# A transposed operand made by VectorE in blocks of 32 and four-way moves through DRAM, where TensorE multiplied by the identity

## The chip, the cores and the metric

The kernel runs on one core of one Trainium2 chip. The metric is the device time of one launch in microseconds (us), and the median of three runs is quoted. TensorE does the matrix products (PE in the rows), VectorE (DVE) and ScalarE (ACT) work elementwise, and SyncE (SP) issues nearly all DMA transfers, in one queue and in program order.

## The reference

One decoder layer with two token mixers, 256 tokens by 2048 features, all in float32. What matters here is its end:

```
ya = jnp.einsum('bsc,cd->bsd', oa * jax.nn.silu(ga), w_o_a[l])
yb = jnp.einsum('bsc,cd->bsd', ob * jax.nn.silu(gb), w_o_b[l])
merged = jax.nn.sigmoid(ma) * ya + jax.nn.sigmoid(mb) * yb
x = x + jnp.einsum('bsd,de->bse', merged, w_out[l])
```

`ya` and `yb` are products over 1024 features, the last product is over all 2048 features of `merged`.

## The kernel before

Every large product is made of **units**. A unit takes two blocks of 128 rows of a weight matrix, 512 columns wide, and multiplies them with both halves (128 tokens each) of the transposed activations. Each float32 operand is split into a high part `hi` and a rest `lo` (both of type fp32r), and hi·hi + hi·lo + lo·hi is added up, so that a unit is 2 x 2 x 3 = 12 products of 128x128 with 128x512. The weights of a unit pass through one of four slots: SP loads `raw` (512 KB), ACT rounds it to `hi`, DVE subtracts to get `lo`, TensorE multiplies. ACT makes `hi` of unit u after the product of unit u-4 is done; DVE makes `lo` of unit u after that; SP loads unit u after the `lo` of unit u-4.

The **tail** of the kernel has 64 units, called 0 to 63 below (the code adds `U_O`). Units 0 to 31 are the two projections, `projections(n)` for column chunk n = 0 to 3: units 8n to 8n+3 for `w_o_a`, 8n+4 to 8n+7 for `w_o_b`. When unit 8n+7 is done, DVE multiplies the second gate in and adds both parts (`gate_b_and_merge(n)`), which gives 512 columns of `merged` in `stage`, tokens on partitions. The last product wants these transposed, features on partitions: `merged_steps` multiplies the eight blocks of 128x128 with the identity on TensorE (into PSUM banks T0 and T0+1), ACT rounds them to `hT_hi` (`merged_hi`), DVE subtracts to `hT_lo` (`merged_lo`). Units 32 to 63 are the product with `w_out`; unit 32+8m+i reads blocks 2i and 2i+1 of `hT_hi` and `hT_lo`, so that chunk n of `merged` is read first by unit 32+2n, and the last chunk (n = 3) by unit 38.

Nothing is scheduled by a planner. Each engine has its own instruction list, written out by hand, and takes it strictly in order; semaphores with a count join them. `split_hi` and `split_lo` count the finished pieces of `hT_hi` and `hT_lo`, `lo_ready` the units whose weights are ready, `unit_done` the finished units.

Of the kernel before, what the change touches and what calls it, by code (L numbers as in the profile page):

```python
# [25 lines left out]
ACT = mybir.ActivationFunctionType  # L26
# [4 lines left out]
P = 128  # L31
# [12 lines left out]
IDX_SCALE = IDX_HEADS ** -0.5 * IDX_DIM ** -0.5  # L44

CW = 512
X_CUTS = (0, 1, 2, 4, 6, 8, 10, 12, 14, 16)
X_FRONT = KT + HD // 2
EARLY = 3
# [84 lines left out]
def build_layer(nc, x, x_columns, positions, w_in, a_q_gain, a_k_gain, b_q_gain, b_k_gain,  # L134
# [4 lines left out]
    with ExitStack() as ctx:  # L139
# [13 lines left out]
        def sem(name):  # L153
            return ctx.enter_context(nc.semaphore(name))
# [64 lines left out]
        swapped = sb("swapped", [P, RT, CW])  # L219
        swapped_r = sb("swapped_r", [P, RT, CW], F32R, at=swapped_at)  # L220

        QB_COLS = 3 * P
        work_flat = [stage[:, :, :].rearrange("p r n -> p (r n)"),
                     roped[:, :, :].rearrange("p r n -> p (r n)"),
# [98 lines left out]
        merged = sem("merged")  # L323
        last_pieces, rest_added = sem("last_pieces"), sem("rest_added")

        dve_wrote = sem("dve_wrote")
# [5 lines left out]
        def _(sp):  # L332
# [64 lines left out]
            def load_projections(n):  # L397

                for b, weights in enumerate((w_o_a, w_o_b)):
                    for i in range(4):  # L400
                        load(i, n * 8 + (U_O + 4 * b + i), weights, 2 * i, n * CW)

            load_projections(0)
            sp.wait_ge(split_lo, 16)
            sp.dma_start(g[:, :, :], x_rows).then_inc(res_landed, 16)
            with sp.Fori(1, 4) as n:
                load_projections(n)
            with sp.Fori(0, 4) as n:
                for i in range(CK):
                    load(i % RING, n * CK + (U_W + i), w_out, 2 * i, n * CW)  # L410
            for n in range(3):
# [103 lines left out]
        def _(pe):  # L515
# [59 lines left out]
            def transpose_step(rows, bank):  # L575

                for b in range(2):
                    for r in range(RT):
                        o = ps[:, bank, b * S + r * P:b * S + (r + 1) * P]
                        ins = nc.tensor.transpose(o.bitcast(F32R), rows(b, r), ident_r[:, :])  # L580
                ins.then_inc(split_T, 1)
# [133 lines left out]
                    w_in_unit(c, i, chunk_bank(c))  # L715


            def merged_steps(n):

                pe.wait_ge(merged, n + 1)  # L720
                pe.wait_ge(split_lo, n * 2 + 16)
                for half in range(2):
                    transpose_step(lambda b, r: stage_r[:, r, (2 * half + b) * P:(2 * half + b + 1) * P], T0 + half)

            def projections(n):

                for branch in range(2):
                    for i in range(4):
                        first = isinstance(n, int)
                        if not first and branch == 0 and i == 2:  # L730
                            merged_steps(n - 1)
# [42 lines left out]
                projections(n)  # L774
            for n in range(4):
                for i in range(CK):
                    if n == 0 and i == 2:
                        merged_steps(3)
                    if i == 0:
                        pe.wait_ge(tail_out, 6 + n + 1)  # L780
                    if n == 0 and i in (0, 6, 7):
                        pe.wait_ge(split_lo, {0: 22, 6: 23, 7: 24}[i])
                    if n < 3 or i < CK - RING:
                        unit(U_W + CK * n + i, i % RING, 2 * i, hT_hi, hT_lo, 2 * (n % 2), i == 0, i == CK - 1)
            last_units()
# [3 lines left out]
        def _(act):  # L789
# [4 lines left out]
            def split_hi_step(t, dst, k0, bank):  # L794

                act.wait_ge(split_T, t - 7)
                activation(dst[:, bass.ds(k0, 2), :], ps[:, bank, :].rearrange("p (k s) -> p k s", k=2),
                           ACT.Copy).then_inc(split_hi, 1)
# [213 lines left out]
            def merged_hi(n, half):  # L1012
                t = n * 2 + half
                split_hi_step(t + 16, hT_hi, t * 2, T0 + half)

            def tail_hi_ahead(n, i):

# [4 lines left out]
                tail_hi_ahead(0, i)  # L1022
            with act.Fori(1, 5) as n:
                for i in range(8):
                    if i in (2, 3):
                        merged_hi(n - 1, i - 2)
                    tail_hi_ahead(n, i)
            for n in range(5, 8):
                for i in range(8):
# [9 lines left out]
        def _(dve):  # L1039
# [290 lines left out]
            def gate_b_and_merge(n):  # L1330

                dve.wait_ge(unit_done, n * 8 + (U_O + 8))
                a_part, b_part = (m[:, :, bass.ds(n * CW + b * D, CW)] for b in range(2))
                tt(b_part, ps[:, 2:4, :], b_part, ALU.mult).then_inc(tail_out, 1)
                dve.wait_ge(tail_out, n * 2 + 2)
                dve.wait_ge(split_T, n * 2 + 8)
                tt(stage[:, :, :], a_part, b_part, ALU.add).then_inc(merged, 1)

            def merged_lo(n, half):
                t = n * 2 + half  # L1340
                split_lo_step(t + 16, hT_lo, hT_hi, t * 2, T0 + half)

            def tail_lo_ahead(n, i):
                make_lo(n * 8 + (U_O + i + RING), i % RING)
# [7 lines left out]
            with dve.Fori(1, 4) as n:  # L1352
                for i in range(8):
                    if i == 0:
                        gate_b_and_merge(n - 1)
                    if i in (2, 3):
                        merged_lo(n - 1, i - 2)
                    if i == 4:
                        gate_a(n)
                    tail_lo_ahead(n, i)  # L1360
            for n in range(4, 8):
                for i in range(8):
                    u = U_O + 8 * n + i
                    if n == 4 and i == 0:
                        gate_b_and_merge(3)
                    if n == 4 and i in (2, 3):
                        merged_lo(3, i - 2)
# [45 lines left out]
```

## Time and profile before

| what | value |
|---|---|
| median of 3 runs | 797.82 us (797.64 to 798.22) |
| span of the profiled execution, first to last instruction | 796.4 us |
| TensorE busy | 792.7 us, 100% of the span |
| VectorE busy | 481.5 us, 60% |
| ScalarE busy | 418.4 us, 53% |
| DMA, mean | 192 GB/s, 152.92 MB |
| granted TensorE clock | 1.000 of full speed throughout |

The span is what the profiler saw between the first and the last instruction. The page gives no other time for this execution; the median of the three runs is 1.4 us above the span, which is what lies outside it. Products overlap in the trace (each is shown with some 390 ns although one starts every 227 ns), so TensorE's rate is read from the distance between starts.

### The profile page before, as it was taken

The numbers are of one execution on the slowest core, as the hardware profiler recorded it, in microseconds if no ns is written. First come the engines' busy times: TensorE is split into PE (matmuls) and PEld (weight loads), VectorE is DVE, ScalarE is ACT, GpSimd is POOL, SyncE is SP. The second block draws the span as 40 slices with busy tenths as digits, with TensorE's granted clock in tenths as the row PEclk, the third lists the DMA queues.
The fourth block names the chain that finished last, engine by engine and source line by source line (L and its number), as shares of the span: only waits on it lengthen the run. The fifth ranks groups of instructions, "written<-read, shape, count | busy, mean of one in ns | idle before, by whom it ended". The sixth has DMA issues, their size and how long they took to land.

```text
span 796.4 us, 10773 instructions
## 1 busy us (share of the span) xinstructions
PE 792.7 (100%) x3810; PEld 667.3 (84%) x3810; DVE 481.5 (60%) x663; ACT 418.4 (53%) x670; POOL 46.8 (6%) x70
## 2 busy tenths in 40 slices
PE   9999999999999999999999999999999999999998
PEld 9998888888888888888888888888888888888887
DVE  7677766666677554668656455555455566665453
ACT  7574556665555454556465554555575444443431
POOL 4341000000000000000000000000000000000000
PEclk9999999999999999999999999999999999999999
DMA  9986665666666565666655665655665855555563
GB/s 316 313 264 198 186 187 168 183 199 180 199 187 187 171 194 162 196 189 193 177 154 173 166 176 161 185 160 172 173 185 182 293 195 184 185 194 189 187 194 122
DMA packets 81082, 152.92 MB, mean 192 GB/s; under 512 B 5136, under 2 KB 12944, under 8 KB 80784
## 3 DMA queue, kind: packets, MB, share of 16 engines
q1 hardware_dynamic: 80752, 152.06, 62.8%
q8 instruction: 25, 0.41, 0.2%
q10 hardware_dynamic: 288, 0.30, 0.1%
q14 instruction: 17, 0.14, 0.0%
HBM read 150.25 MB, written 2.10 MB: 191 GB/s over the span
## 4 chain that ended last, share of the span: by engine, by line
PE 97%; ACT 1%; DMA 1%; SPq 0%; issue 0%; DVE 0%; ACTq 0%
PE ps L527 30%; PE ps L529 30%; PE ps L528 29%; PE ps L538 2%; PE ps L569 1%; PE ps L580 1%; DMA raw<-in_w_in 1%; PE ps L638 0%; PE ps L749 0%; PE ps L748 0%; PE ps L747 0%; PE ps L646 0%; ACT L938 0%; ACT L832 0%; ACT g L832 0%; PE ps L626 0%
## 5 line engine op out<-in xcount | busy, mean ns | idle before, releaser
L1068 DVE TENSOR_TENSOR lo<-raw,hi 128x1024 fp32r<-128x1024 f32 (+2 forms) x279 | 335.2, 1204 | 290.2 <-ACT hi L819 288.4
L819 ACT ACTIVATE hi<-raw 128x1024 fp32r<-128x1024 f32 (+2 forms) x277 | 287.1, 1040 | 337.4 <-PE ps L529 323.8
L527 PE MATMUL ps<-hi,hT_hi 128*128 128x512 f32 (+2 forms) x936 | 364.3, 389 | 0.0
L529 PE MATMUL ps<-hi,hT_lo 128*128 128x512 f32 (+2 forms) x936 | 361.1, 386 | 0.0
L528 PE MATMUL ps<-lo,hT_hi 128*128 128x512 f32 (+2 forms) x936 | 360.8, 385 | 0.0
L529 PEld LDWEIGHTS ps<-hi,hT_lo 128*128 128x128 f32 x936 | 175.7, 188 | 35.1
L528 PEld LDWEIGHTS ps<-lo,hT_hi 128*128 128x128 f32 x936 | 175.8, 188 | 32.9
L527 PEld LDWEIGHTS ps<-hi,hT_hi 128*128 128x128 f32 x936 | 175.7, 188 | 33.0
L527 PE MATMUL ps<-hi,ogT_hi 128*128 128x512 f32 x128 | 50.1, 391 | 0.0
L529 PE MATMUL ps<-hi,ogT_lo 128*128 128x512 f32 x128 | 49.8, 389 | 0.0
L528 PE MATMUL ps<-lo,ogT_hi 128*128 128x512 f32 x128 | 49.8, 389 | 0.0
L453 POOL TENSOR_SCALAR small<-small 128x8 f32<-128x8 f32 (+1 forms) x13 | 2.8, 212 | 504.2 <-ACT stage L999 318.4
L529 PEld LDWEIGHTS ps<-hi,ogT_lo 128*128 128x128 f32 x128 | 24.0, 188 | 5.0
L528 PEld LDWEIGHTS ps<-lo,ogT_hi 128*128 128x128 f32 x128 | 24.0, 188 | 4.9
L527 PEld LDWEIGHTS ps<-hi,ogT_hi 128*128 128x128 f32 x128 | 24.0, 188 | 4.9
L938 ACT ACTIVATE roped<-stage,small 128x128 f32<-128x128 f32 (+1 forms) x32 | 14.3, 446 | 13.0 <-DVE small L1206 13.0
L856 ACT ACTIVATE swapped<-stage 128x128 f32<-128x128 f32 x64 | 18.9, 297 | 0.3
L455 POOL TENSOR_TENSOR small<-small,half 128x8 f32<-128x8 f32 (+1 forms) x13 | 16.6, 1281 | 1.1
L1088 DVE TENSOR_TENSOR swapped<-stage,g 128x256 f32<-128x256 f32 (+2 forms) x44 | 16.2, 409 | 0.0
L1084 DVE TENSOR_TENSOR roped<-stage,g 128x512 f32<-128x512 f32 (+2 forms) x22 | 14.5, 660 | 0.0
L1092 DVE TENSOR_TENSOR roped<-roped,swapped 128x1024 f32<-128x1024 f32 (+2 forms) x11 | 12.3, 1121 | 0.0
L856 ACT ACTIVATION_READ_ACCUMULATOR swapped<-stage 128x1 f32 x64 | 12.0, 188 | 0.0
(167 smaller groups left out, 484.5 us busy)
## 6 DMA issues: line engine op xcount, KB each, us to landing
raw<-in_w_in SPq DMA_DIRECT2D x192, 512.0 KB, 3.8
raw<-in_w_out SPq DMA_DIRECT2D x32, 512.0 KB, 4.3
raw<-in_w_o_a SPq DMA_DIRECT2D x16, 512.0 KB, 3.7
raw<-in_w_o_b SPq DMA_DIRECT2D x16, 512.0 KB, 3.6
raw<-in_w_in SPq DMA_DIRECT2D x13, 384.0 KB, 5.3
raw<-in_w_in SPq DMA_DIRECT2D x8, 336.0 KB, 5.3
x_own<-in_x SPq DMA_DIRECT2D x4, 512.0 KB, 6.4
g<-in_x SPq DMA_DIRECT2D x1, 2048.0 KB, 10.3
```

What stands on the lines that cost most here:

```text
L455: return tt(out, mean, half[:, 0:width], ALU.pow)
L527: mm(o, a_hi, w_hi[:, j], start=first and j == 0, stop=False)
L528: mm(o, a_hi, w_lo[:, j], start=False, stop=False)
L529: ins = mm(o, a_lo, w_hi[:, j], start=False, stop=j == 1 and last)
L538: ins = mm(ps[:, chunk_bank(c) + r, 0:IDX_W[0]], stationary[:, 2 * unit_k + j, r * P:(r + 1) * P], moving[:, u % RING, j, 0:IDX_W[0]], sta ...
L819: activation(hi[:, slot, :, 0:width], raw[:, slot, :, 0:width], ACT.Copy).then_inc(hi_ready, 1)
L856: ins = activation(swapped[:, r, at], stage[:, r, at], ACT.Square, accum_out=ss_h[:, j:j + 1])
L938: ins = activation(probs[buf][:, at], masked[buf][:, at], ACT.Exp, scale=SCALE, bias=neg_max[:, j:j + 1], accum_out=sum_p[:, j:j + 1])
L1068: tt(lo[:, slot, :, 0:width], raw[:, slot, :, 0:width], hi[:, slot, :, 0:width].bitcast(F32), ALU.subtract).then_inc(lo_ready, 1)
L1084: mark(tt(cos_out[:, r], src[:, r], c_tab, ALU.mult))
L1088: mark(tt(sin_out[:, r, :, half_b], src[:, r, :, other], s_tab, ALU.mult))
L1092: tt(roped[:, :, 0:cols], roped[:, :, 0:cols], swapped[:, :, 0:cols], ALU.add).then_inc(rope_done, 1)
```

## The change

The eight identity products for each chunk, their PSUM banks and `merged_steps` go. After the sum, DVE transposes `stage` in blocks of 32x32 into `swapped` (one instruction over 128x1024). SP then writes `swapped` to a DRAM buffer (`keep_turned`, 512 KB), waits until it has landed, and reads it back in four transfers of 128 KB, one for each group of 32 partitions, in runs of 256 numbers, into `roped` (`bring_turned`). ACT and DVE make `hT_hi` and `hT_lo` from `roped`, in two pieces of 128x512 (one for each half of the tokens), before they turn to the weights of unit 8n+8 (for chunk n-1), i.e. two places later in their lists than before.

```diff
+            def keep_turned(n):
+                sp.wait_ge(merged_turned, n + 1)
+                sp.dma_start(turned_home, swapped[:, :, :].rearrange("p r n -> p (r n)")).then_inc(turned_kept, 16)
+
+            def bring_turned(n):
+                sp.wait_ge(turned_kept, 16 * n + 16)
+                for c in range(P // BLOCK):
+                    to = roped[c * BLOCK:(c + 1) * BLOCK, :, :].rearrange("j r n -> j (r n)")
+                    sp.dma_start(to.rearrange("j (q n) -> j q n", q=P // BLOCK), turned_rows[c]).then_inc(turned_back, 16)
+
+            def move_merged(n, i):
+                if n >= 0 and i == 0:
+                    keep_turned(n)
+                if n >= 0 and i == 1:
+                    bring_turned(n)
...
-            def merged_steps(n):
-
-                pe.wait_ge(merged, n + 1)
-                pe.wait_ge(split_lo, n * 2 + 16)
-                for half in range(2):
-                    transpose_step(lambda b, r: stage_r[:, r, (2 * half + b) * P:(2 * half + b + 1) * P], T0 + half)
-
...
-                    if n == 0 and i in (0, 6, 7):
-                        pe.wait_ge(split_lo, {0: 22, 6: 23, 7: 24}[i])
+                    if n == 0 and i in (0, 4, 6):
+                        pe.wait_ge(split_lo, {0: 20, 4: 22, 6: 24}[i])
...
+            def merged_hi(n):
+
+                act.wait_ge(turned_back, 64 * n + 64)
+                for r in range(RT):
+                    to = hT_hi[:, bass.ds(n * 4, 4), r * P:(r + 1) * P]
+                    activation(by_blocks(to), columns_of(roped, r), ACT.Copy).then_inc(split_hi, 1)
...
-                    if i in (2, 3):
-                        merged_hi(n - 1, i - 2)
+                    if i == 4:
+                        merged_hi(n - 1)
...
                 dve.wait_ge(tail_out, n * 2 + 2)
-                dve.wait_ge(split_T, n * 2 + 8)
                 tt(stage[:, :, :], a_part, b_part, ALU.add).then_inc(merged, 1)
+                dve.wait_ge(merged, n + 1)
+                nc.vector.transpose(swapped[:, :, :].rearrange("p r n -> p (r n)"),
+                                    blocks_of(stage)).then_inc(merged_turned, 1)
+
+            def merged_lo(n):
+
+                for r in range(RT):
+                    dve.wait_ge(split_hi, n * 2 + (17 + r))
+                    to, rounded = (t[:, bass.ds(n * 4, 4), r * P:(r + 1) * P] for t in (hT_lo, hT_hi))
+                    tt(by_blocks(to), columns_of(roped, r), by_blocks(rounded).bitcast(F32),
+                       ALU.subtract).then_inc(split_lo, 1)
```

SP's list, which was three loops over the tail, is now written out. These are its rows from the loads of units 32 and on, for the chunks n = 2 and n = 3. Before, two loads in a row of one loop (the wait, then the transfer):

```order
L353 ISA [waits lo_ready]
L353 DMA raw<-in_w_out 128x2x512
L351 REGISTER_ALU
L353 ISA [waits lo_ready]
L353 DMA raw<-in_w_out 128x2x512
```

And now, from the load of unit 32 to those after the last block move:

```order
L371 DMA raw<-in_w_out 128x2x512 [waits lo_ready]
L424 DMA turned<-swapped 128x1024 [waits merged_turned]
L371 DMA raw<-in_w_out 128x2x512 [waits lo_ready]
L430 DMA roped<-turned 32x4x256 [waits turned_kept]
L430 DMA roped<-turned 32x4x256 x3
L371 DMA raw<-in_w_out 128x2x512 [waits lo_ready] x7
L424 DMA turned<-swapped 128x1024 [waits merged_turned]
L371 DMA raw<-in_w_out 128x2x512 [waits lo_ready]
L430 DMA roped<-turned 32x4x256 [waits turned_kept]
L430 DMA roped<-turned 32x4x256 x3
L371 DMA raw<-in_w_out 128x2x512 [waits lo_ready] x22
```

For chunk 3 the write stands behind the load of unit 40, and the four reads behind the load of unit 41; the load of unit 42 stands behind them.

VectorE's list for the last chunk, from the gate product of chunk 3 on. Before:

```order
L1334 TENSOR_TENSOR m<-ps,m 128x2x512 [waits unit_done]
L1337 TENSOR_TENSOR stage<-m 128x1024 [waits split_T,tail_out]
L1068 TENSOR_TENSOR lo<-raw,hi 128x1024 [waits hi_ready] x2
L1054 TENSOR_TENSOR hT_lo<-ps,hT_hi 128x512 [waits split_hi]
L1068 TENSOR_TENSOR lo<-raw,hi 128x1024 [waits hi_ready]
L1054 TENSOR_TENSOR hT_lo<-ps,hT_hi 128x512 [waits split_hi]
L1068 TENSOR_TENSOR lo<-raw,hi 128x1024 [waits hi_ready] x5
```

And now:

```order
L1363 TENSOR_TENSOR m<-ps,m 128x2x512 [waits unit_done]
L1365 TENSOR_TENSOR stage<-m 128x1024 [waits tail_out]
L1367 STREAM_TRANSPOSE swapped<-stage 128x1024 [waits merged]
L1097 TENSOR_TENSOR lo<-raw,hi 128x1024 [waits hi_ready] x4
L1375 TENSOR_TENSOR hT_lo<-roped,hT_hi 128x4x128 [waits split_hi] x2
L1097 TENSOR_TENSOR lo<-raw,hi 128x1024 [waits hi_ready] x4
```

The block transpose stands ahead of the `lo` of unit 36, and both pieces of `hT_lo` between the `lo` of unit 39 and that of unit 40.

## Rows read from the trace of the kernel before

**Rows 1.** The page: the chain that ended last, by engine.

```profile
span 796.4 us, 10773 instructions
PE 792.7 (100%) x3810; PEld 667.3 (84%) x3810; DVE 481.5 (60%) x663; ACT 418.4 (53%) x670; POOL 46.8 (6%) x70
PE 97%; ACT 1%; DMA 1%; SPq 0%; issue 0%; DVE 0%; ACTq 0%
```

**Rows 2.** Timeline of TensorE, last chunk: start, duration, line, operation.

```profile
705.61 0.39 PE L527 MATMUL ps<-hi,hT_hi 128*128 128x512 f32 x1
...
711.06 0.81 PE L580 MATMUL ps<-ident_r,stage_r 128*128 128x128 f32 x8
...
718.61 0.39 PE L527 MATMUL ps<-hi,hT_hi 128*128 128x512 f32 x1
...
721.33 0.39 PE L527 MATMUL ps<-hi,hT_hi 128*128 128x512 f32 x1
...
722.69 0.39 PE L527 MATMUL ps<-hi,hT_hi 128*128 128x512 f32 x1
```

**Rows 3.** The chain in order of time: start, duration; first and last of four.

```profile
643.69 0.64 PE ps L580 x8
...
711.22 0.65 PE ps L580 x8
```

**Rows 4.** Timeline of VectorE around the last chunk.

```profile
706.90 1.23 DVE L1068 TENSOR_TENSOR lo<-raw,hi 128x1024 fp32r<-128x1024 f32 x1 [1.49 <-ACT hi L819]
708.05 1.22 DVE L1334 TENSOR_TENSOR m<-ps,m 128x1024 f32<-128x1024 f32 x1
709.30 1.23 DVE L1337 TENSOR_TENSOR stage<-m 128x1024 f32<-128x1024 f32 x1
710.44 1.22 DVE L1068 TENSOR_TENSOR lo<-raw,hi 128x1024 fp32r<-128x1024 f32 x1
...
716.97 0.68 DVE L1054 TENSOR_TENSOR hT_lo<-ps,hT_hi 128x512 fp32r<-128x512 f32 x1
```

**Rows 5.** Timeline of ScalarE around the last chunk.

```profile
711.25 1.06 ACT L819 ACTIVATE hi<-raw 128x1024 fp32r<-128x1024 f32 x1 [1.66 <-PE ps L529]
712.22 0.58 ACT L797 ACTIVATE hT_hi<-ps 128x512 f32 x1
```

**Rows 6.** Timeline of SP's queue: the issues of loads 40 and 41.

```profile
711.83 0.38 SPq L353 DMA_DIRECT2D raw<-in_w_out  x1
...
713.75 0.37 SPq L353 DMA_DIRECT2D raw<-in_w_out  x1
```

**Rows 7.** Instructions of tile raw, 705 to 740 us: the 13 loads, issue to landing.

```profile
DMA to landing us min/median/max: 3.4/4.2/4.5
```

**Rows 8.** DMA issues from 755 us on: count, KB each, us to landing.

```profile
out<-g SPq DMA_DIRECT2D x1, 256.0 KB, 2.2
...
out<-g SPq DMA_DIRECT2D x1, 128.0 KB, 1.9
```

**Rows 9.** DMA issues from 774 to 775.5 us, and from 775.5 to 777 us.

```profile
raw<-in_w_out SPq DMA_DIRECT2D x1, 512.0 KB, 5.0
out<-g SPq DMA_DIRECT2D x1, 512.0 KB, 5.2
...
out<-g SPq DMA_DIRECT2D x1, 512.0 KB, 6.1
```

**Rows 10.** Busy time by stretch: us, PE, PEld, DVE, ACT, POOL, clock, DMA share, GB/s.

```profile
4.00:10.00 6.00, 5.92 (x32) 5.49 (x32) 4.40 (x9) 4.27 (x10) 0.00 (x0) 1.00 1.01 341
793.00:794.00 1.00, 0.64 (x6) 0.44 (x4) 0.74 (x2) 0.00 (x0) 0.00 (x0) 1.00 0.00 0
794.00:795.00 1.00, 0.00 (x0) 0.00 (x0) 0.11 (x1) 0.00 (x0) 0.00 (x0) 1.00 0.40 136
795.00:796.00 1.00, 0.00 (x0) 0.00 (x0) 0.00 (x0) 0.00 (x0) 0.00 (x0) 1.00 0.37 126
```

**Rows 11.** Busy time, 688 to 710 us, the 22 us before the last chunk.

```profile
688.00:710.00 22.00, 22.00 (x104) 18.24 (x103) 14.09 (x14) 9.46 (x10) 0.00 (x0) 1.00 0.54 181
```

More of the change, by code:

```diff
@@ L46 @@
 CW = 512
+BLOCK = 32
 X_CUTS = (0, 1, 2, 4, 6, 8, 10, 12, 14, 16)
@@ L220, in build_layer, with blocks_of, columns_of, by_blocks @@
         swapped_r = sb("swapped_r", [P, RT, CW], F32R, at=swapped_at)
+        turned_home = nc.dram_tensor("turned", (P, RT * CW), F32, kind="Internal").ap()
+        turned_rows = turned_home.rearrange("(q j) (c n) -> c j q n", j=BLOCK, c=P // BLOCK)
+        def blocks_of(t):
+            return t[:, :, :].rearrange("p r (b c i) -> p c (r b) i", c=P // BLOCK, i=BLOCK)
+        def columns_of(t, r):
+            return t[:, :, :].rearrange("p r n -> p (r n)").rearrange("p (q r b i) -> p r b q i", q=P // BLOCK, r=RT,
+                                                                      i=BLOCK)[:, r]
+        def by_blocks(t):
+            return t.rearrange("p b (q i) -> p b q i", i=BLOCK)
         QB_COLS = 3 * P
@@ L322, in build_layer @@
         gates_ready = sem("gates_ready")
-        merged = sem("merged")
+        merged, merged_turned, turned_kept, turned_back = (sem("merged"), sem("merged_turned"), sem("turned_kept"),
+                                                           sem("turned_back"))
         last_pieces, rest_added = sem("last_pieces"), sem("rest_added")
@@ L401, in load_projections @@
                         load(i, n * 8 + (U_O + 4 * b + i), weights, 2 * i, n * CW)
+                        move_merged(n - 2, 4 * b + i)
+            def keep_turned(n):
[11 more added lines that the diff above has]
+                    bring_turned(n)
             load_projections(0)
@@ L405, in _ @@
             sp.dma_start(g[:, :, :], x_rows).then_inc(res_landed, 16)
-            with sp.Fori(1, 4) as n:
+            for n in range(1, 4):
                 load_projections(n)
-            with sp.Fori(0, 4) as n:
+            for n in range(4):
                 for i in range(CK):
                     load(i % RING, n * CK + (U_W + i), w_out, 2 * i, n * CW)
+                    if n < 2:
+                        move_merged(n + 2, i)
             for n in range(3):
@@ L729, in projections @@
                         first = isinstance(n, int)
-                        if not first and branch == 0 and i == 2:
-                            merged_steps(n - 1)
                         if i == 0 and first:
@@ L776, in _ @@
                 for i in range(CK):
-                    if n == 0 and i == 2:
-                        merged_steps(3)
                     if i == 0:
                         pe.wait_ge(tail_out, 6 + n + 1)
-                    if n == 0 and i in (0, 6, 7):
-                        pe.wait_ge(split_lo, {0: 22, 6: 23, 7: 24}[i])
+                    if n == 0 and i in (0, 4, 6):
+                        pe.wait_ge(split_lo, {0: 20, 4: 22, 6: 24}[i])
                     if n < 3 or i < CK - RING:
@@ L1010, in _ @@
                     make_hi_ahead(c, i)
-            def merged_hi(n, half):
-                t = n * 2 + half
-                split_hi_step(t + 16, hT_hi, t * 2, T0 + half)
+            def merged_hi(n):
[3 more added lines that the diff above has]
+                    activation(by_blocks(to), columns_of(roped, r), ACT.Copy).then_inc(split_hi, 1)
             def tail_hi_ahead(n, i):
@@ L1335, in gate_b_and_merge @@
                 dve.wait_ge(tail_out, n * 2 + 2)
-                dve.wait_ge(split_T, n * 2 + 8)
                 tt(stage[:, :, :], a_part, b_part, ALU.add).then_inc(merged, 1)
-            def merged_lo(n, half):
-                t = n * 2 + half
-                split_lo_step(t + 16, hT_lo, hT_hi, t * 2, T0 + half)
+                dve.wait_ge(merged, n + 1)
[7 more added lines that the diff above has]
+                       ALU.subtract).then_inc(split_lo, 1)
             def tail_lo_ahead(n, i):
@@ L1355, in _ @@
                         gate_b_and_merge(n - 1)
-                    if i in (2, 3):
-                        merged_lo(n - 1, i - 2)
                     if i == 4:
                         gate_a(n)
+                        merged_lo(n - 1)
                     tail_lo_ahead(n, i)
@@ L1365, in _ @@
                         gate_b_and_merge(3)
-                    if n == 4 and i in (2, 3):
-                        merged_lo(3, i - 2)
+                    if n == 4 and i == 4:
+                        merged_lo(3)
                     if n >= 5 and i == 0:
```

## Prediction

> **What bounds the kernel now.** I read the page first: TensorE is busy 100% of the span and carries 97% of the chain that ended last [rows 1]. So time is saved only by taking work out of TensorE's stream, and lost only where TensorE is made to wait. Next I read TensorE's own timeline in the tail for its pace. A unit of 12 products starts at 718.61 and the next at 721.33 [rows 2]: 2.72 us a unit, 227 ns a product, with no gap. Then the other engines in the last iteration before the change's critical place: over 22 us VectorE is busy 14.09, ScalarE 9.46, the DMA engines 54% [rows 11]. Each has room on average; whether the new chain of steps fits is a question of its length, not of these shares.
>
> **What is taken away.** Eight identity products for each of four chunks. The chain gives them 0.64 to 0.65 us for eight [rows 3], but the products behind them are also paced a little slower for a while. The honest price is the distance between repeats. The first and last of the four groups start at 643.69 and 711.22 [rows 3]: 67.53 us for three iterations, 22.51 each, where eight units take 8 x 2.72 = 21.76. So a group costs 0.75 us, and four give back **3.0 us**. They do lie on the path, since nothing else is on TensorE at those times. The same comes out at the last group: unit 32 starts at 705.61, so unit 38 would start at 705.61 + 6 x 2.72 = 721.93, and it starts at 722.69 [rows 2], 0.76 later.
>
> The Trainium skill (VectorE: DVE Perf Modes, Rules for kernel authors and The three transpose paths) speaks against the change: transpose 128x128 blocks on TensorE if the result may lie in PSUM, as it did here. Its figure for one such product on TensorE is 390 ns, for bf16. By it 32 products would cost 12.5 us, and the kernel would come out near 788 with the stall below. The starts in rows 2 and 3 are closer than that by four times (0.65 us for eight), so I give that outcome no more than 0.01.
>
> **What is added, and who waits for it.** A chain: block transpose on VectorE, write to DRAM, read back, `hT_hi`, `hT_lo`, and then TensorE. For the chunks n = 0 to 2 TensorE reads the result an iteration or more later, so their latency itself is hidden. The last chunk is first read by unit 38, six units after the sum can begin. That is the place where the end is set. I write it in the times of the trace before, with unit 32 starting at T = 705.61 [rows 2]; the three groups saved earlier only shift T.
>
> 1. VectorE: `lo` of unit 35 from 706.90, gate product 708.05, sum 709.30 to 710.53 [rows 4], as before.
> 2. Block transpose. No row shows one. The nearest are VectorE's operations over 128x1024 f32, 1.22 us [rows 4]. I take 1.2, with a start 0.1 after the sum ends: done at 711.85. Bounds: 0.6 if it ran at twice that pace, 2.4 if it took two passes.
> 3. `lo` of unit 36 follows, to 713.1 instead of 710.44 + 1.22 = 711.66. SP issues the load of unit 40 behind it; before, this came 0.17 after the end of `lo` (711.83) and took 0.38 [rows 6]. So the load goes out at 713.25 and the write, next in the queue, at 713.65. The wait for `merged_turned` is long over by then. The load of unit 41 moves from 713.75 [rows 6] to some 714.4; it is not late, since its `hi` waits for unit 37.
> 4. Write of 512 KB. Two rows with less and nothing ahead of them: 1.9 us for 128 KB, 2.2 for 256 KB [rows 8], which at 0.3 for each 128 KB makes 2.8 for 512 KB. Of full size, right behind a load as here: 5.2, and 6.1 with another write ahead [rows 9]. I take 4.8, a little under the row that is nearest, since the load ahead of that one was itself slow (5.0 against a median of 4.2 [rows 7]). Landed at 718.45; bounds 2.8 and 6.1.
> 5. Four reads of 128 KB, issued from 718.55. SP needs some 0.35 for each issue (0.37 for a load [rows 6]), so the last goes out 1.05 after the first. Loads of 512 KB in one piece land after 3.4 to 4.5, median 4.2 [rows 7]. The runs are 1 KB, where the write's are 4 KB; but runs of 1.5 KB at the kernel's start still moved 341 GB/s [rows 10], so I don't slow them, and take 4.2: all four landed at 722.75. Bounds 3.4, and 5.1 if the moved bytes (half of a load's time) took twice as long.
> 6. ScalarE: two copies of 128x512, 0.58 each [rows 5], 722.85 to 724.0. VectorE: the second `hT_lo` behind it, 0.68 [rows 4], to **724.75**. Both engines are free: the `lo` of unit 39 is done by some T + 13.5.
>
> TensorE wants unit 38's operands at 721.93. It stands still for **2.8 us**. Sum: -3.0 + 2.8 = -0.2 us. Against the profiled execution: 796.4 - 0.2 = 796.2 of span, and with the 1.4 us by which the median stands above that span 797.6.
>
> **What is queued behind the waits.** SP waits at the first read for the write to land, up to 718.55, and issues the four reads to 719.9. Loads 42 and 43 stand behind; 42 goes out at 719.9. Its `hi` may begin when unit 38 is done, after 724.6 and now later still, and 719.9 + 4.2 = 724.1: not late. ScalarE waits for the reads before the `hi` of unit 40. Here is the second place: in the iterations n = 1 to 3 the same wait stands ahead of the `hi` of unit 8n+8, which TensorE wants 8 units = 21.76 us after T. Reads landed at T + 17.14, two copies (1.15), `hi` of unit 8n+8 (1.06), `lo` (1.23) and the hand-overs: ready at T + 20.65. **Slack 1.1 us.** The unit after it has 2.72 more to spend and costs ScalarE 1.06, so it has no stall. I cost this place at nothing; the cover is this 1.1 us, and every microsecond beyond it costs one in each of three iterations besides the one at unit 38. VectorE's transposes themselves (4 x 1.2) are hidden in its idle time; the block product delays the `lo` of unit 8n+4 by 1.3, which TensorE wants at T + 10.9 and which is done at T + 7.5. The chunk's gates are read from PSUM before the transpose, so no bank comes free later. The unrolled loops of SP cost nothing on TensorE's path.
>
> **The clock.** Granted clock is 1.00 to the end [rows 10], which is the 2.4 GHz level. After the last product at 793.6 TensorE does nothing, and the clock still stands at 1.00 in the slice up to 796.00, 2.4 us later. A stall of 2.8 us is about as far as any row reaches. If it fell to 1.2 GHz behind the stall, each unit at that level would take up to 5.4 instead of 2.72; one such unit would add 2.7 us. That belongs to the slower outcomes.
>
> **The rivals.**
>
> - *No change that can be told, as above:* a stall of 1.4 to 4.6 us at unit 38 against 3.0 saved, 796.2 to 799.4. A difference under 0.2% (1.6 us) is about what a measurement of this kernel can't tell from none. Chance 0.51.
> - *Faster, transfers are quick:* both land at the ends nearest to what a transfer can do alone. Write 3.4 (2.8 and 0.6 for the load ahead), reads 3.4: the end is 2.2 us earlier, the stall 0.6, and the sum -2.4: 795.4. It decides when the two transfers together take less than 7.6 us. For it: loads landed in as little as 3.4 (the lowest of rows 7); against it: the write follows a load by 0.4 us, and four separate reads must all land. Chance 0.15. The Trainium skill (DMA: Bandwidth & Descriptors, Anatomy of one DMA) gives about 2.0 us fixed and then 436 GB/s, for transfers that GpSimd issues. By it 512 KB take 3.2 us, both 6.4 instead of 9.0; the stall would be 0.2 us and the median 795.0. In this tail no load of 512 KB landed in less than 3.4 [rows 7] and no write of that size in less than 5.2 [rows 9].
> - *Slower, ScalarE's wait for the block reads starves TensorE in every iteration:* write 6.1 and reads 5.1, landed at T + 19.3. Then `lo` of unit 8n+8 is ready at T + 22.8, 1.1 us late in each of three iterations, and unit 38 waits 5.0: -3.0 + 3.3 + 5.0 = +5.3, 803.1. It starts to count from T + 18.2 and turns the result slower by 0.2% when the reads land some 1.3 us later than I take, at T + 18.4 (-0.2 + 1.3 + 3 x 0.2 = +1.7). For it: six hand-overs between engines and queues, of which I gave most 0.1 us or nothing; 1 KB pieces; loads, write and reads share one queue at 54% load. Chance 0.27.
> - *Slower, one term is larger:* the block transpose takes 2.4 (everything is 1.2 later, stall 4.0, and the slack overdrawn by 0.1 in three iterations: +1.3), and with it the clock falls for a unit or two: 799 to 802. Chance 0.06.
> - *The identity products were not worth their distance:* TensorE's stream is no shorter without them, because the same time goes to something that they hid. The stall then stands alone: +2.8, 800.6. Nothing in rows 2 shows such cover. Chance 0.01.
>
> **How the numbers follow.** The likeliest is the sum, 797.6. Its own range is 796.2 to 799.4. The range that should hold 8 of 10 reaches down to the quick transfers, 795.4, and up into the starved iterations, short of their far end: 802.0. Faster 0.15, same 0.51, slower 0.34 (0.27 + 0.06 + 0.01).
>
> **What the profile after would show.** Identity products on `stage` gone, four iterations 21.76 us apart (22.51 before) if no stall is in them. One gap on TensorE before unit 38, released by VectorE's `hT_lo`, of 2 to 4 us. Block transpose about 1.2 us. Write landing in 4.8, the reads in 4.2 from the first issue. ScalarE's longest wait in the tail for `roped`, near 5 us in each iteration. The prediction fails if the transfers take under 7.6 or over 10.3 us together, or if the `hi` of unit 8n+8 comes so late that TensorE also waits at the start of an iteration.

## The result and the profile after

The changed kernel takes 803.15 us (median of 4, 802.72 to 804.86) against 797.73 us before (median of 4): ratio 1.0071, 95% interval 1.0057 to 1.0086. It is 5.4 us slower; the forecast was no change, with a range that ended at 802.0. The profiled execution is the longest of the four: 804.86 us, span 803.0. The one before was the longest of its four too: 798.22 us, span 796.4 [rows 1].

The page after, its busy times, the granted clock by fortieths of the span, the chain that ended last, and TensorE's idle time in two groups (behind the bar: busy, mean ns of one; then the idle time before them and its releaser):

```profile
span 803.0 us, 10549 instructions
PE 793.4 (99%) x3778; PEld 666.5 (83%) x3778; DVE 485.9 (61%) x667; ACT 417.9 (52%) x670; POOL 46.8 (6%) x70
PEclk9999999999999999999999999999999999998999
PE 87%; DMA 5%; DVE 3%; ACT 2%; issue 2%; SPq 1%; DVEq 0%; ACTq 0%
L564 PE MATMUL ps<-hi,hT_hi 128*128 128x512 f32 (+2 forms) x936 | 365.7, 391 | 4.2 <-DVE hT_lo L1375 4.0
L564 PE MATMUL ps<-hi,ogT_hi 128*128 128x512 f32 x128 | 50.0, 391 | 1.6 <-DVE lo L1097 1.6
```

TensorE held 97% of the chain before; now 87%, and DMA 5%. One slice of the clock is lower. The first product of the tail, all gaps of TensorE in it and the products around the last one, from its timeline (start, duration, in brackets the idle time before and what ended it):

```profile
615.97 0.39 PE L564 MATMUL ps<-hi,ogT_hi 128*128 128x512 f32 x1
...
661.10 0.50 PE L564 MATMUL ps<-hi,ogT_hi 128*128 128x512 f32 x1 [1.45 <-DVE lo L1097]
...
683.32 0.50 PE L564 MATMUL ps<-hi,ogT_hi 128*128 128x512 f32 x1 [0.16 <-DVE lo L1097]
...
705.66 0.47 PE L564 MATMUL ps<-hi,hT_hi 128*128 128x512 f32 x1 [0.28 <-DVE lo L1097]
...
721.87 0.39 PE L566 MATMUL ps<-hi,hT_lo 128*128 128x512 f32 x1
726.21 0.80 PE L564 MATMUL ps<-hi,hT_hi 128*128 128x512 f32 x1 [3.95 <-DVE hT_lo L1375]
726.81 0.63 PE L565 MATMUL ps<-lo,hT_hi 128*128 128x512 f32 x1
727.23 0.63 PE L566 MATMUL ps<-hi,hT_lo 128*128 128x512 f32 x1
...
732.35 0.41 PE L566 MATMUL ps<-hi,hT_lo 128*128 128x512 f32 x1
732.60 0.40 PE L564 MATMUL ps<-hi,hT_hi 128*128 128x512 f32 x1
```

The reader is to see three things. First, the three gaps at the starts of units 16, 24 and 32 have used up what three groups of identity products gave back (2.25 us): unit 32 starts at 705.66, before at 705.61 [rows 2]. The brackets give 1.89 us for the three, but they count from the modelled end of the product before, 0.39 after its start, where the next product would start after 0.227. By the starts, units 0 to 31 took 89.69 us here (615.97 to 705.66) and 87.04 in the kernel without the trip, shown below: 2.65 lost. Second, the gap at unit 38: without it this unit would start 0.23 after 721.87, at 722.10; it starts at 726.21, 4.1 later. Third, behind the gap the products start 0.60 and then 0.42 to 0.43 apart instead of 0.227, until 732.35. Busy times by stretch (the third column from the right is the clock) say why:

```profile
724.00:726.00 2.00, 0.00 (x0) 0.00 (x0) 1.13 (x2) 1.80 (x3) 0.00 (x0) 0.88 0.99 347
726.00:728.00 2.00, 1.79 (x4) 1.49 (x5) 1.83 (x3) 1.25 (x2) 0.00 (x0) 0.50 0.28 100
728.00:730.00 2.00, 2.00 (x6) 1.52 (x5) 0.69 (x1) 0.00 (x0) 0.00 (x0) 0.50 0.58 187
730.00:732.00 2.00, 2.00 (x6) 1.52 (x6) 0.00 (x0) 0.26 (x1) 0.00 (x0) 0.50 0.82 259
732.00:734.00 2.00, 2.00 (x10) 1.62 (x9) 1.17 (x1) 0.80 (x1) 0.00 (x0) 0.91 0.20 78
```

The granted clock fell to 0.50 (1.2 GHz) while TensorE stood idle. From 726.21 to 732.60 fifteen products start; at 0.227 each that takes 3.4 us, here 6.39: **3.0 us** lost to the clock and the first product behind the gap. The account of this execution, all by starts: -3.0 (products gone) + 2.8 (gaps at iterations: 2.65, and 0.1 behind the start of unit 32, whose next product also comes late) + 4.1 + 3.0 - 0.4 (the tail began earlier, at 615.97 instead of 616.33) = +6.5. The last product starts 6.5 later than before (799.88, before 793.37), and the span is 6.6 longer.

The chain in order of time, from the sum of chunk 1 to the copies of chunk 3, with the longest pieces only (start, length, what):

```profile
665.73 1.24 DVE stage L1365
...
668.15 1.20 DVE lo L1097
669.78 5.75 DMA turned<-swapped
675.92 0.43 SPq L430
...
676.87 2.91 DMA roped<-turned
680.44 0.62 ACT hT_hi L1043
681.06 0.96 ACT hi L845
...
691.99 5.81 DMA turned<-swapped
...
714.14 5.73 DMA turned<-swapped
...
721.21 2.87 DMA roped<-turned
724.20 0.64 ACT hT_hi L1043
724.87 1.30 DVE hT_lo L1375 x2
```

The writes go out at 669.78, 691.99 and 714.14, some 22.2 us apart, where eight units take 21.76. (The first went out at 645.62, 24.2 before the second: its four reads took 6.4 us from the first issue to the copies, the other chunks' 4.3.) It is a loop of its own: the reads land, ScalarE and VectorE catch up on four units of weights, only then VectorE multiplies the next gate in, sums, transposes, and the next write goes out. The block transpose itself takes what was assumed:

```profile
704.29 4.63 DVE L1097 TENSOR_TENSOR lo<-raw,hi 128x1024 fp32r<-128x1024 f32 x4
708.84 1.22 DVE L1363 TENSOR_TENSOR m<-ps,m 128x1024 f32<-128x1024 f32 x1
710.09 1.23 DVE L1365 TENSOR_TENSOR stage<-m 128x1024 f32<-128x1024 f32 x1
711.34 1.25 DVE L1367 STREAM_TRANSPOSE swapped<-stage 128x1024 f32<-128x1024 f32 x1
```

### The profile page after: what moved, and what is told of

The parts are those of the page before. It is cut to its first block, busy times and chain, and to the rows that moved or that the text cites. A ratio compares the mean times of both kernels' runs of the same rounds, so it can differ in the third digit from the quotient of the medians.

```text
span 803.0 us, 10549 instructions
## 1 busy us (share of the span) xinstructions
PE 793.4 (99%) x3778; PEld 666.5 (83%) x3778; DVE 485.9 (61%) x667; ACT 417.9 (52%) x670; POOL 46.8 (6%) x70
## 4 chain that ended last, share of the span: by engine, by line
PE 87%; DMA 5%; DVE 3%; ACT 2%; issue 2%; SPq 1%; DVEq 0%; ACTq 0%
PE ps L564 26%; PE ps L566 26%; PE ps L565 26%; DMA turned<-swapped 3%; PE ps L575 3%; DMA roped<-turned 2%; DVE lo L1097 2%; PE ps L606 1%; ACT hi L845 1%; DVE stage L1365 1%; SPq L430 1%; DVE m L1363 1%; PE ps L623 1%; PE ps L675 0%; PE ps L777 0%
## 5 line engine op out<-in xcount | busy, mean ns | idle before, releaser
L1043 ACT ACTIVATE hT_hi<-roped 128x512 f32 x8 | 4.6, 624 | 27.2 <-DMA roped<-turned 27.2
L1375 DVE TENSOR_TENSOR hT_lo<-roped,hT_hi 128x512 f32 (+1 forms) x8 | 5.2, 688 | 21.8 <-ACT hT_hi L1043 21.8
```

## The experiments

Each is an edit of the changed kernel; times are medians, and ratios are to the kernel before, run on the same chip beside them (797.73, 798.27 and 798.15 us in the three groups of four). Differences to the changed kernel are to its 803.15 us; since the kernel before differs by up to 0.5 us between groups, they are no more exact than that, and the ratios go before them.

**Without the trip.** Left out are the write and the reads; the copies come from the block-transposed tile.

```diff
...
-                act.wait_ge(turned_back, 64 * n + 64)
+                act.wait_ge(merged_turned, n + 1)
...
-                    activation(by_blocks(to), columns_of(roped, r), ACT.Copy).then_inc(split_hi, 1)
+                    activation(by_blocks(to), columns_of(swapped, r), ACT.Copy).then_inc(split_hi, 1)
...
```

> The write and the four reads are left out; ScalarE and VectorE take their copies from the block-transposed tile itself, so blocks are not moved between partition groups and the last product works on wrongly placed numbers. Theory: the identity products are worth 3.0 us of TensorE's stream (four groups of 0.75), VectorE's block transposes are hidden, and all of the loss comes from the trip through DRAM. Then no TensorE gap is left in the tail, iterations are 21.76 us apart and the time is 797.7 - 3.0 = 794.7 (794.2 to 795.3). Rival: the stream without identity products is not shorter, or VectorE's transposes delay the weights: 797.5 or more, with gaps on TensorE behind lo.

Measured: 794.99 us, ratio 0.9965 (0.9952 to 0.9979). No gap of TensorE in the tail; the span is 793.4, 3.0 less than before (the medians differ by 2.7). Units 0 to 31 take 87.04 us, 32 times 2.72:

```profile
616.36 0.39 PE L561 MATMUL ps<-hi,ogT_hi 128*128 128x512 f32 x1
...
703.40 0.39 PE L561 MATMUL ps<-hi,hT_hi 128*128 128x512 f32 x1
```

The products were worth 3.0 us, and VectorE's transposes cost nothing. Everything lost is lost by the trip.

**The gap at unit 38 filled.** 18 products that nobody reads.

```diff
+                    if n == 0 and i == 6:
+                        for _ in range(18):
+                            mm(ps[:, T0, :], hT_hi[:, 0, 0:P], hT_hi[:, 0:2, :], start=True, stop=True)
                     if n == 0 and i in (0, 4, 6):
```

> 18 products of 128x128 with 128x512 into a PSUM bank that nobody reads are put on TensorE ahead of unit 38, which fill 18 x 0.227 = 4.1 us, the length of the gap there. Theory: behind the gap TensorE ran at 1.2 GHz for 14 products of 0.427 instead of 0.227 us, 2.8 us in all, and the first product after the gap took 0.37 longer; with the gap filled the granted clock stays at 1.00, and the time falls by 2 to 3.2 us to 800 to 801. Rival: only the wait itself costs, and the low clock is no more than a sign of it (or comes in any case): time as in the changed kernel, 803.1, or some tenths more.

Measured: 800.92 us (800.32 to 801.66), 2.2 less than the changed kernel; ratio 1.0038 (1.0025 to 1.0052). TensorE still waited after the filling, and the clock stayed up:

```profile
720.46 4.24 PE L809 MATMUL ps<-hT_hi 128*128 128x512 f32 x18
725.91 0.50 PE L564 MATMUL ps<-hi,hT_hi 128*128 128x512 f32 x1 [1.21 <-DVE hT_lo L1378]
```

So the low clock is a cost of its own, 2 to 3 us on top of the gap: 2.2 by the medians here, 3.0 by the starts in the profiled execution of the changed kernel. In this execution the last chunk's reads took 5.95 us and not 4.3, so that unit 38 waited longer than in the changed kernel (from 720.46 to 725.91, the filling counted in) and the clock still held. The Trainium skill (TensorE: Matmul & The Clock Gate, Why this matters for your kernels) warns of idle gaps between bursts of products, behind which, if they are long, the clock is back at half; the rows agree: it fell in a gap of 3.95 us and stayed up over the 1.21 that the filling left.

**Reads behind two more loads.**

```diff
-                if n >= 0 and i == 1:
+                if n >= 0 and i == 3:
                     bring_turned(n)
```

> SP issues the four block reads behind the loads of units 8n+10 and 8n+11 instead of ahead of them; they still go out soon after the write has landed. Theory: in the changed kernel the fourth read landed after 4.9 us where the first three took 2.7 to 2.9, because two loads of 512 KB are issued right behind it; with nothing behind the reads the fourth takes 2.8 to 3.2, all have landed some 4.5 us after the first issue instead of 6.3, the stall at unit 38 shrinks from 4.0 to about 2.2, the iterations' stalls go, and the time is 799 to 801. Rival: the reads are slow by themselves (1 KB rows, half of the partitions' ports), or the two loads, now ahead of them, cost them the same: 803 or later.

Measured: 816.61 us, ratio 1.0235 (1.0221 to 1.0249), 13.5 slower than the changed kernel. My theory for this run fell. I had read the fourth read's 4.9 us as the doing of the loads issued behind it; but that was the first chunk's, and in the other three the fourth read landed in 2.9 with the same loads behind it (the chain above). SP's queue and then ScalarE in one iteration of this kernel:

```profile
698.62 0.47 SPq L424 DMA_DIRECT2D turned<-swapped  x1
699.35 4.53 SPq L371 DMA_DIRECT2D raw<-in_w_out  x3
704.14 1.75 SPq L430 DMA_DIRECT2D roped<-turned  x4
```

```profile
711.23 1.15 ACT L1043 ACTIVATE hT_hi<-roped 128x512 f32 x2 [9.00 <-DMA roped<-turned]
```

From the first issue (704.14) to the last landing (711.2) 7.1 us pass, where the changed kernel needs 4.3 in three of its four chunks. What is *ahead* in the queue delays the reads: with three loads issued just ahead of them they took 6.8 to 8.0 us in the four chunks, though none was issued behind them before they had landed.

**Copies one place later.**

```diff
-                    if i == 4:
+                    if i == 5:
                         merged_hi(n - 1)
...
                         gate_a(n)
+                    if i == 5:
                         merged_lo(n - 1)
...
-                    if n == 4 and i == 4:
+                    if n == 4 and i == 5:
                         merged_lo(3)
```

> ScalarE's and VectorE's copies of the returned blocks stand one place later, behind hi and lo of unit 8n+8 instead of ahead of them. Theory: ScalarE's wait of up to 7.8 us for the reads no longer holds up the weights of unit 8n+8, so the gaps at the starts of iterations (1.45, 0.16, 0.28 us) go, and the write of the last chunk goes out 0.5 to 0.8 earlier; the stall at unit 38 stays, at 3.2 to 3.9. Time 800 to 801.3. Rival: the iterations' gaps come from late loads (SP's wait for the write ahead of loads 8n+10 and on), and stay: 802.5 to 803.5.

Measured: 800.95 us, 2.2 less; ratio 1.0038 (1.0024 to 1.0052). The gaps at iterations are gone; the one at unit 38 stays at its size, 3.0 us earlier than in the changed kernel:

```profile
723.25 0.80 PE L564 MATMUL ps<-hi,hT_hi 128*128 128x512 f32 x1 [3.94 <-DVE hT_lo L1375]
```

The gaps at iterations came from the place of the copies in two lists, not from late loads. The first chunk's reads took 6.4 us here too, and one place later in the lists that cost TensorE nothing.

**Write ahead of the load.**

```diff
+                        if b == 0 and i == 0 and n >= 2:
+                            keep_turned(n - 2)
                         load(i, n * 8 + (U_O + 4 * b + i), weights, 2 * i, n * CW)
...
-                if n >= 0 and i == 0:
-                    keep_turned(n)
...
+                    if n < 2 and i == 0:
+                        keep_turned(n + 2)
                     load(i % RING, n * CK + (U_W + i), w_out, 2 * i, n * CW)
```

> The write is issued ahead of the load of unit 8n+8 instead of behind it. Theory: it goes out when the block transpose is done, 1.5 to 2 us sooner, with no load ahead of it; the reads follow, the iterations' gaps go (1.9 us in all), the stall at unit 38 falls from 4.0 to 2.0 to 2.5, and the clock may stay up. Time 797 to 799.5. Rival: the write takes its 5.7 us whatever is ahead of it and the reads now meet the load behind it (6 us or more from first issue to last landing): a gain of 1.5 us or less, 801 or later.

Measured: 802.61 us (801.71 to 805.32), ratio 1.0061 (1.0047 to 1.0076) against 1.0071 (1.0057 to 1.0086): no gain that can be told from none, the rival's outcome by its own second reason. SP's queue in one iteration, then ScalarE:

```profile
688.75 0.34 SPq L426 DMA_DIRECT2D turned<-swapped  x1
689.85 1.50 SPq L371 DMA_DIRECT2D raw<-in_w_out  x2
692.32 1.96 SPq L432 DMA_DIRECT2D roped<-turned  x4
```

```profile
701.49 1.15 ACT L1045 ACTIVATE hT_hi<-roped 128x512 f32 x2 [7.62 <-DMA roped<-turned]
```

The reads could be issued 3.6 us after the write (in the first chunk 2.8, the value that I had worked out for a write with nothing ahead), not 5.8. But then they took 9.2 us instead of 4.3 (8.1 to 9.2 in the four chunks), and two loads now stand directly ahead of them. From the issue of the write to the copies 12.7 us pass here and 10.2 in the changed kernel (in the last chunk 11.8 and 10.1), so that what the write gained the reads lost, and more. The run with the reads behind two more loads says the same: the reads wait for the loads that stand ahead of them. No run issued them from another queue.

**Another order for the last product.** Its first two column chunks take the block pairs 0 to 5 each, then 6 and 7 each. The residual of the first column chunk is added six units later, since this chunk is finished later.

```diff
+OUT_ORDER = ([(m, i) for m in range(2) for i in range(6)] + [(m, i) for m in range(2) for i in (6, 7)]
+             + [(m, i) for m in (2, 3) for i in range(8)])
...
-            for n in range(4):
-                for i in range(CK):
...
+            for at, (n, i) in enumerate(OUT_ORDER):
...
-                    if n >= 5 and i == 0:
+                    if n == 5 and i == 6:
+                        add_residual(u, 0)
+                    if n >= 6 and i == 0:
```

> Only the order of the last product changes: its first two column chunks take their six early pairs of blocks each (12 units) before the pairs that need the last chunk of merged, so that this is first read by unit 44 instead of 38, 16.3 us later. Theory: the stall at unit 38 goes, with it the low clock, and what stays is 3.0 saved against the iterations' gaps of 1.9: 797.7 - 1.1 = 796.6 (795.8 to 797.2). Rival: part of the time after the gap is lost to something else than the missing operands (late loads behind the reads): 798 or later, with gaps on TensorE behind lo at units 40 to 43.

Measured: 797.22 us against 798.27, ratio 0.9988 (0.9979 to 0.9996), 1.05 us faster than before; 1.1 was expected. The gap before the last chunk's blocks and the low clock are gone, and gaps of 0.59 us at unit 16 and 0.74 at unit 40, behind `lo`, are left.

**Both edits: order and later copies.**

```diff
...
+            for at, (n, i) in enumerate(OUT_ORDER):
...
-                    if i == 4:
+                    if i == 5:
                         merged_hi(n - 1)
...
```

> The two edits together: new order of the last product, and the copies of the returned blocks one place later on ScalarE and VectorE. Theory: both kinds of gap are gone, all of the 3.0 us is kept, and the time is that of the kernel without the trip, 794.7 to 795.2, faster than both kernels. Rival: the trip costs something besides its two waits (transfers that slow the loads, VectorE's work): 796 or later.

Measured: 795.15 us (794.95 to 795.63) against 798.27, ratio 0.9962 (0.9949 to 0.9975). This is faster than both kernels, by 3.1 and by 8 us, and by its ratio as fast as the kernel without the trip (0.9965, 0.9952 to 0.9979). Its page:

```profile
span 793.3 us, 10549 instructions
PEclk9999999999999999999999999999999999999999
PE 97%; ACT 1%; DMA 0%; issue 0%; SPq 0%; DVE 0%; ACTq 0%
```

The transfers still take their time (the last chunk's write goes out at 710.92 and its copies begin at 721.47), but nobody waits for them. The chain is TensorE's again.

**Half of the reads.** Left out is one half of the returned numbers.

```diff
-sp.dma_start(to.rearrange("j (q n) -> j q n", q=P // BLOCK), turned_rows[c])
+sp.dma_start(to.rearrange("j (q n) -> j q n", q=P // BLOCK)[:, 0:2], turned_rows[c][:, 0:2])
```

> Each of the four block reads brings only two of its four block rows, so half of the returned numbers are left out and the last product works on old contents there. Theory: the reads are limited by the bytes or rows moved, 256 KB less at 190 to 260 GB/s, so all have landed 1.0 to 1.4 us sooner, the stall at unit 38 and the iterations' gaps shrink by that: time 800 to 801.5. Rival: the reads cost four issues of 0.43 us and a fixed latency, whatever they carry: 802.5 to 803.3.

Measured: 798.03 us (797.57 to 799.44), ratio 1.0003 (0.9994 to 1.0012), 5.1 less than the changed kernel, more than I expected. The reads took 3.5 us in each chunk, where full ones took 4.3 (and 6.4 in the first chunk); 0.85 us for 256 KB, some 300 GB/s. The rest of the gain has two parts. In the profiled execution no gap was left at the starts of iterations (2.8 us in the changed kernel's), and the clock stayed up: the gap at unit 38 was 2.23, and in 7 of 11 runs the mean granted clock was 1.0.

**Pieces or partitions.** Three ways to move the same bytes otherwise. Whole rows of 4 KB in four reads (blocks land in wrong places):

```diff
+sp.dma_start(to, turned_home[c * BLOCK:(c + 1) * BLOCK, :]).then_inc(turned_back, 16)
```

> The four reads bring the same 128 KB each into the same 32 partitions, but whole rows of 4 KB of the DRAM buffer instead of four pieces of 1 KB from four rows; the blocks are then in the wrong places. Theory S (small pieces): the pieces of 1 KB make the reads slow (6.3 us from first issue to last landing, and 2.8 less with half of them); whole rows land after 4 to 4.8 us, the clock may stay up, 798.5 to 801. Theory P (partitions): a transfer into 32 partitions is slow by itself, whatever its pieces: 802.5 to 803.5.

One read into 128 partitions, pieces of 1 KB (blocks land in wrong places):

```diff
...
+pieces = turned_home.rearrange("p n -> (p n)").rearrange("(q p n) -> p q n", q=4, p=P)
+to = roped[:, :, :].rearrange("p r n -> p (r n)").rearrange("p (q n) -> p q n", q=4)
+sp.dma_start(to, pieces).then_inc(turned_back, 64)
```

> One read of 512 KB into all 128 partitions, in pieces of 1 KB (one for each partition and block row), instead of four reads into 32 partitions each; the blocks are then in the wrong places. Theory S (small pieces): still slow, all landed 5 to 6 us after the issue, 801.5 to 803. Theory P (partitions, or four issues): landed after 3.5 to 4.5, 798 to 800.5.

Four writes with pieces of 1 KB, one read of whole rows:

```diff
...
+for q in range(P // BLOCK):
+    own = swapped[q * BLOCK:(q + 1) * BLOCK, :, :].rearrange("j r n -> j (r n)")
+    sp.dma_start(turned_rows[q], own.rearrange("j (c n) -> j c n", c=P // BLOCK)).then_inc(turned_kept, 16)
...
+sp.dma_start(roped[:, :, :].rearrange("p r n -> p (r n)"), turned_home).then_inc(turned_back, 16)
```

> The same result by the mirror image: four writes of 128 KB, each from 32 partitions in pieces of 1 KB, and one read of 512 KB in rows of 4 KB. Theory S: the writes now take 6 us or more and the read 4, a sum of 10 to 11 instead of 12, and 800 to 802.5. Theory P: the same if reading from and writing to 32 partitions are alike. If small pieces are slow only when DRAM is read, the writes take 5.7 as before and the sum is 9.5 to 10: 798 to 800.

| kernel | first issue to copies, last chunk | gap at unit 38 | clock, range of the runs | median us (ratio) |
|---|---|---|---|---|
| changed | 4.3 | 3.95 | 0.996 to 0.998 | 803.15 (1.0071) |
| whole rows | 4.2 | 3.58 | 0.996 to 0.998 | 801.57 (1.0045) |
| one read | 3.9 | 2.61 | 0.996 to 1.000 | 800.61 (1.0032) |
| four writes | 4.4 | 3.34 | 0.996 to 1.000 | 801.10 (1.0035) |

Neither theory S nor theory P holds as the reason for slow reads. Both were drawn up against the 6.3 us of the first chunk, and the other three chunks' reads took 4.3 in the changed kernel already. Whole rows give 0.1 us, one read instead of four 0.4 us, and four writes take about as long as one (5.3 to 5.6 against 5.7 to 5.8). The times differ by more than that. In the profiled executions of "whole rows" and "one read" the first chunk's reads took 4.1 and 3.9 us and not 6.4, and no gap at an iteration is left; "four writes" has one of 0.47. And each of these kernels stands near the point where the clock falls. The six runs of "one read" lie apart by it: 797.99 and 799.13 us at clock 1.000, and 799.94 to 801.95 at 0.996 to 0.998; whether they differ in the iterations too is not shown, since only one was profiled. Its profiled run, the 797.99, kept the clock over a gap of 2.61:

```profile
722.24 0.50 PE L564 MATMUL ps<-hi,hT_hi 128*128 128x512 f32 x1 [2.61 <-DVE hT_lo L1375]
```

**No DRAM buffer.** 16 transfers between partition groups.

```diff
...
+for c in range(P // BLOCK):
+    for q in range(P // BLOCK):
...
+        sp.dma_start(to[:, q * 256:(q + 1) * 256], own[:, c * 256:(c + 1) * 256]).then_inc(turned_back, 16)
```

> No DRAM buffer: 16 transfers of 32 KB, each from one group of 32 partitions straight to another, issued where the write stood. Theory: one latency instead of two, 512 KB moved instead of 1 MB; 16 issues at 0.33 to 0.43 us take 5.3 to 6.9, the last lands 2 to 3 after that, 8 to 10 us after the first issue instead of 12. The stall at unit 38 falls to 0.5 to 2.5, the iterations' gaps go, the clock stays up: 795 to 798. Rival: many small transfers in one queue are slower than two trips (a completion for each, pieces of 1 KB): 801 or later.

Measured: 812.06 us, ratio 1.0178 (1.0161 to 1.0195). The last chunk's 16 issues took 10.0 us of SP's queue (721.30 to 731.31), 0.63 each and not 0.33 to 0.43, and the copies began 11.4 after the first. That is 1.3 longer than the way through DRAM (10.1 from the issue of the write at 714.14 to the copies at 724.20), and SP could issue no load in those 10 us. The rival was right. The first gap of this execution, at unit 16, is the shortest behind which the clock fell:

```profile
661.77 0.50 PE L565 MATMUL ps<-hi,ogT_hi 128*128 128x512 f32 x1 [2.12 <-DVE lo L1098]
...
663.00:665.00 2.00, 2.00 (x6) 1.54 (x6) 1.89 (x2) 1.73 (x2) 0.00 (x0) 0.50 0.82 283
```

## Why the prediction was wrong

**What was right.** The 3.0 us for the products (span 793.4 without the trip). The place of the stall, unit 38, and its releaser, `hT_lo`. The block transpose, 1.25 for 1.2. The reads, 4.3 for 4.2 in three of four chunks. The rival of the starved iterations gave 803.1 with a chance of 0.27, and 803.15 was measured; that the number fits is luck, for its parts were others: it had 3.3 for the iterations and 5.0 at unit 38 and no clock, where the profiled execution had 2.8, 4.1 and 3.0.

**What the sum lacked.** It gave -0.2, and the profiled execution had +6.5. Of the 6.7 between them 2.8 are the iterations, priced at nothing; 1.3 the stall at unit 38, 4.1 and not 2.8; 3.0 the clock, priced at nothing; and the tail began 0.4 earlier.

**Step 4, the write.** I took 4.8, "a little under the row that is nearest"; it was 5.7 to 5.8 in every chunk of the changed kernel. The nearest row said 5.2 and its neighbour 6.1 [rows 9]. Here a load stood ahead of the write and another was issued 0.7 us behind it. By this term come 0.95 of the 1.4 us by which the last chunk was later than forecast (`hT_lo` done 20.5 after the start of unit 32, not 19.1).

**The slack of 1.1 us, "I cost this place at nothing".** This step failed in kind. I compared `lo` of unit 8n+8 with TensorE's need for it, and let the units behind it pass. But VectorE's list has four `lo` behind the wait and then the gate product of the same chunk: after the copies it worked without a pause from 704.29 to 713.7, and the gate product began at 708.84, 3.2 after the start of unit 32, instead of 2.44 before (708.05 [rows 4] against 705.61). So each chunk's write went out later because the chunk before had been late; the loop of 22.2 us is what the account of slack could not show. The rest of the 1.4 us, 0.4, is this: the write went out 8.5 after the start of unit 32, not 8.0. The copies one place later cut the loop, and 2.2 us came back. Not all of the 2.8 us is the loop: 1.7 were lost at unit 16, behind the first chunk, whose write and reads together took 12.1 us (5.7 and 6.4), far over the 10.3 at which the prediction had the iterations starve. The next two stayed under it, at 10.1 and 10.2, and still had gaps, at units 24 and 32. With the gap filled and all of the first three chunks' reads at 4.3 to 4.4 us, the writes went out 22.1 to 22.4 apart all the same, and units 0 to 31 lost 0.9 us (616.12 to 704.02, 87.90). So the loop cost about 0.9, and the slow first reads made it 2.7.

**The clock.** I had set the stall at 2.8 us, next to the 2.4 us over which a row showed the clock to stay up, and left its fall to the outliers with one unit at half pace. At a real stall of 4.1 it fell in every run of the changed kernel (0.996 to 0.998), and cost 3.0 us in the profiled one, as much as the whole gain of the change. Filling the gap showed 2.2 us in the medians. A stall estimated near a point where something else tips should have been priced with both branches in the sum.

**What stays open.** Why one chunk's four reads were slow in some executions, with the same four issues. The first chunk's took 6.4 us in three (changed kernel, copies later, both edits) and 4.3 to 4.4 in two (gap filled, new order); the last chunk's took 5.95 and 5.2 in these two, and 5.1 with both edits. Only one execution of each kernel was profiled, so how often this happens isn't known, nor how much of the spread of a kernel's runs it makes.

## What to carry to other kernels

A transfer that moved off the busiest engine is paid for by the distance between its producer and its first reader, so look first for an order that lengthens that distance: here 12 units of the last product instead of 6 could be taken ahead of the first that needs the late blocks, and together with the later copies the change turned from 5.4 us slower to 3.1 faster. Where a late result stands in an in-order list, follow what is queued behind it all the way round to the next start of the same chain, since a loop slightly longer than the iteration eats every slack. And on one DMA queue count the bytes ahead, not the latencies: putting the write first only moved the same wait to the reads.

## What the runs showed of the hardware

- The granted clock stayed at 1.00 over gaps of 2.23 and 2.61 us, and of 2.12 and 2.72 in the run with the reads behind two more loads. It fell to 0.50 in gaps of 2.87, 3.27, 3.58, 3.81, 3.94, 3.95, 4.22 and 6.89 us, and shortly behind the end of gaps of 3.34 (four writes) and 2.12 (no DRAM buffer). So a gap of 2.1 to 2.9 us did either, and so did executions of one kernel (one read: 1.000 in two of six runs). Once down, it stood at 0.50 for some 7 us in the changed kernel, "copies later" and "whole rows", for some 3 in "write ahead of the load" and "four writes", and for some 10 around the gap of 6.89.
- VectorE's block transpose of 128x1024 f32 took 1.25 us, as much as a sum of that size (1.23).
- A write of 512 KB to DRAM behind one load took 5.7 to 5.8 us in the changed kernel (5.3 to 6.1 in six other kernels, and once 6.8 with the new order); with nothing ahead, the next transfer that waited for it went out after 2.8 to 3.6 us.
- Reads of 512 KB from DRAM, from the first issue to the copies: four into 32 partitions each in pieces of 1 KB 4.3 us, the same in pieces of 4 KB 4.2, one into 128 partitions in pieces of 1 KB 3.9; with two or three loads just ahead of them, 6.8 to 9.2. Sixteen transfers of 32 KB between partition groups: 11.4 us, at 0.63 us for each issue (12.7 in the first chunk).
